# A two-block network on one core: transfers and first splits in another order, layer norm about a provisional mean, attention's last steps by head

## The chip, the cores and the metric

The kernel runs on one core of one Trainium2 chip. The metric is the device time in microseconds of one execution; the median over the runs is what is compared.

## The reference, cut to what matters

Input `x` is 256 tokens by 1024 features, in float32. Three stages follow one another: a block with a Conformer convolution, a SwiGLU feed-forward and a gated side input; a block with differential attention, feed-forward and side input; and a third block with a spatial gate, a pooling branch and a short convolution. All matrices are multiplied as split products (below). The change touches the first input norm, the convolution's layer norm and the end of attention:

```python
def layer_norm(x, g, b):
    mu = jnp.mean(xf, axis=-1, keepdims=True)
    xc = xf - mu
    var = jnp.mean(xc * xc, axis=-1, keepdims=True)
    y = xc * lax.rsqrt(var + EPS) * g + b
def conformer_conv(x, w_pw1, b_pw1, dw_w, dw_b, ln_g, ln_b, w_pw2, b_pw2):
    a = x @ w_pw1 + b_pw1
    u = a[..., :D_MODEL] * jax.nn.sigmoid(a[..., D_MODEL:])
    u = causal_depthwise_conv_31_taps(u, dw_w) + dw_b
    u = jax.nn.silu(layer_norm(u, ln_g, ln_b))
    return u @ w_pw2 + b_pw2
# attention, per head: w = softmax_0 - lam * softmax_1;  out = w @ v;  rms_norm(out) @ w_o
```

## The kernel before, in words

**Weights.** 169 pieces of 1 MB (128 partitions x 2048 float32) are streamed by SyncE into the four buffers `raw` (loop at L235 to L240). A piece `g` may be loaded when the split of piece `g-4` is done. Each piece is split in two parts: ScalarE writes `w_hi` (rounded to fp32r, `feed`, L936) and VectorE writes `w_lo = raw - w_hi` (L1424); GpSimd does this for the pieces in `POOL_LO` (`low`, L818). Each product is three TensorE matmuls, hi*hi, hi*lo and lo*hi (`mm3`, L282 to L284). `ahead` and `feed` write the order of the splits out by hand between the other steps of ScalarE and VectorE; each engine runs its instructions in program order and waits on semaphores.

**Start.** SyncE issues the two loads of `h` (the input, one per 128 tokens, L234) and then the weight pieces. ScalarE issues the load of `prm` (all per-feature parameters), squares `h` for the norm (L1065), GpSimd computes the factor (L805, L806), ScalarE scales the first half of the tokens (L1069) and VectorE the second (L1584). ScalarE then issues the two loads of `p_feat`. TensorE fills its wait with 23 dummy matmuls (`keep_busy`, L456), transposes the scaled tokens (L324), VectorE applies the gain (L1469), ScalarE and VectorE split it in `x_hi` (L954) and `x_lo` (L1479). Piece 0 is split in halves: first half `w_hi` by ScalarE (L1073), `w_lo` by VectorE (L1588); second half by ScalarE (L1075) and GpSimd (L825). The product `first_piece` has two halves in the same way, over features 0 to 511 and 512 to 1023.

**Convolution.** Features 0 to 511 (four blocks) are convolved on VectorE (31 instructions a block, `taps_on_vector`), with sums in bank 6; the other four on TensorE (`conv_taps`, L499), from rows spread through memory. The results are `y[:, 0..7, :]`, features on partitions, tokens along the row.

**Layer norm.** The mean over features is a matmul with the constant matrix `inv_d` (1/1024 everywhere): the sum of blocks 0, 1, 2 and 4 (`y_part`, made by GpSimd, L844 to L849) goes first (L522), blocks 5, 6, 3, 7 follow one by one (`mean_of`, L509). VectorE subtracts the mean from all blocks, two at a time (L1650); ScalarE squares them (L1143); eight matmuls on quadrants sum the squares (L536), VectorE copies (L1654), two matmuls of one column make the variance (L544), VectorE adds epsilon (L1657), GpSimd takes the power -1/2 (L865), VectorE makes diagonals (L1660), TensorE spreads them in a row (L550), VectorE multiplies (`scaled`, L1666), ScalarE applies Silu and rounds (L1151, L1156), VectorE forms `z_lo` (`v_split`, L1674), and `by_feature` begins the product with `pw2`. Four parts of the side input's projection (`projection_part`, 6 matmuls each) and six `keep_warm` transposes (L449) stand between these steps on TensorE. GpSimd, in the order of its program: splits of pieces 8, 9 and 10 with the sums for `y_part`, four additions of the bias row to `h` (L857), the store of the attention bias `toep` (L862), then the power.

**Attention's end.** For head `hd`: `logits`, VectorE `masked` (L1739) and `mix` (L1747 to L1754), ScalarE's exponentials (L1209), transposed weights (`weights`, L614) that ScalarE copies (L1215), and `values` for a pair of heads (L629 to L631), which VectorE evacuates (L1761). Squares of the outputs (L1229), GpSimd's power (L893, L894), `o_norm`, transposes (`o_jobs`), and the splits (L1236, L1780) go ahead of the product with `wo`.

Of the kernel before, what the change touches and what calls it, by code (L numbers as in the profile page):

```python
# [15 lines left out]
P = 128  # L16
# [61 lines left out]
def build(nc, ws, x_tok, p_feat, par, rows, lam_rows, rel, onehot, sgu_w, pool_m, toep, u_scr, out):  # L78
    ctx = ExitStack()
    with ctx:  # L80
# [174 lines left out]
        def _(pe):  # L255
# [93 lines left out]

            def projection_part(layer, g, b, t, n):  # L350

                begin(b)
                for k in range(2):
                    c = slice(k * D + n * 512, k * D + (n + 1) * 512)
                    ins = mm3(banks[b][:, :], tok(z_hi, KB - 2 + k, t), tok(z_lo, KB - 2 + k, t),
                              w_hi[:, g % SPLIT, c], w_lo[:, g % SPLIT, c], k == 0, k == 1)
                end(("proj", layer, t, n), b, ins, g if t == 1 and n == 1 else None)
# [101 lines left out]
            keep_busy(23, 7)  # L459
# [43 lines left out]
            def mean_of(f, last=False):  # L503

                if f < CONV_PE:
                    pe.wait_ge(S("conv"), f + 1)
                else:
                    pe.wait_ge(S("conv_pe"), f - CONV_PE + 1)
                ins = pe.matmul(banks[0][:, 0:SEQ], inv_d, y[:, f, :], start=False, stop=last)  # L509
                if last:  # L510
                    end("mean", 0, ins, release=(S("centred"), 4))
# [21 lines left out]
            for f in range(KB):  # L533
                pe.wait_ge(S("y_sq"), f // 2 + 1)
                j = f % QUADS
                ins = pe.matmul(banks[7][j * LANE:(j + 1) * LANE, 0:SEQ], inv_d[:, 0:LANE], sq[:, f, :],  # L536
                                start=f < QUADS, stop=f >= QUADS)
            end("squares", 7, ins, release=(S("y_sums"), 1))
            pe.wait_ge(S("y_sums"), 1)
            pe.wait_ge(S("one_32nd"), 1)  # L540
            begin(3)
            begin(2)
            for t, b in enumerate((3, 2)):
                end(("var", t), b, pe.matmul(banks[b][:, 0:1], y_sums[:, t * P:(t + 1) * P], one_32nd, start=True, stop=True),  # L544
                    release=(S("y_var"), t + 1))
            projection_part(0, G["proj0"], 5, 1, 0)
# [5 lines left out]
            projection_part(0, G["proj0"], 6, 1, 1)  # L552
            keep_warm(6, 7)
# [64 lines left out]
            def values(pair):  # L618

                def go():  # L620
# [32 lines left out]
            for step in (values(0), weights(5), weights(6), values(1), weights(7), values(2), values(3)):  # L653
                step()
# [129 lines left out]
        def _(pool):  # L784
# [11 lines left out]
            pool.memset(inv_d, 1.0 / D).then_inc(S("consts"), 1)  # L796
            pool.memset(u_pad[:, :, TAPS - 1 + SEQ:PADDED], 0.0)
# [4 lines left out]
            pool.dma_start(lam_t[:, :, :], bass.AP(lam_rows.tensor, 0, [[0, P], [HD, 4], [1, HD]])).then_inc(S("ld_lam"), 16)  # L802

# [11 lines left out]
            def low(g):  # L815
# [7 lines left out]
            pool.wait_ge(S("first_lo_a"), 1)  # L823
            pool.wait_ge(hi_done, 1)
            pool.tensor_tensor(w_lo[:, 0, D:HALF], raw[:, 0, D:HALF], w_hi[:, 0, D:HALF].bitcast(F32), ALU.subtract) \  # L825
                .then_inc(S("first_lo_b"), 1)
            pool.wait_ge(lo_done, 1)
# [26 lines left out]
            for n_ in range(2):  # L854
                for t in range(TT):
                    c = slice(n_ * 512, (n_ + 1) * 512)
                    pool.tensor_tensor(h[:, t, c], h[:, t, c], row_b2[:, c], ALU.add).then_inc(S("h_biased"), 1)  # L857


            pool.wait_ge(S("bias_row"), 2)  # L860
            pool.wait_ge(S("ld_u0"), 128)
            pool.dma_start(toep, bias_row[:, :].unsqueeze(1).to_broadcast([HEADS, P, 384])).then_inc(S("toep_out"), 16)  # L862
            pool.memset(one_32nd, 1.0 / LANE).then_inc(S("one_32nd"), 1)
            pool.wait_ge(S("y_var"), 2)
            pool.tensor_tensor(st[:, 84:86], st[:, 82:84], st2[:, 56:58], ALU.pow).then_inc(S("y_r"), 1)  # L865
            pool.wait_ge(S("h_done"), 4)
# [59 lines left out]
        def _(act):  # L926
# [133 lines left out]
            act.dma_start(prm[:, :], par).then_inc(S("ld_par"), 16)  # L1060
# [15 lines left out]
            fed[0] = 1  # L1076
            feed(1)
            h_split("x", 1)
            feed(2)

            def sigmoid(f):

# [1048 lines left out]
```

## Time and profile before

| | |
|---|---|
| runs | 1038.81, 1035.30, 1035.13 us; median 1035.3 |
| profiled execution | 1035.07 us, of which the span is 1033.3 |
| TensorE busy | 1022.6 us (99%) |
| VectorE / ScalarE / GpSimd busy | 638.0 / 517.7 / 109.5 us |
| chain that ended last | TensorE 97% of it |
| read from memory | 187.58 MB, 185 GB/s over the span |

A TensorE row of the timeline is a group of matmuls; a float32 matmul shows as two records (x2). Busy time of TensorE overlaps from one matmul to the next, so that starts are more telling than durations. "[0.65 <-DVE ...]" at the end of a row is the idle time of that engine before it, and what ended it.

### The profile page before, as it was taken

How to read it: one execution, taken by the hardware profiler on the slowest of the kernel's cores; microseconds unless marked ns; L12 is line 12 of the kernel's file. 1: busy time of each engine (PE TensorE's matmuls, PEld its weight loads, DVE VectorE, ACT ScalarE, POOL GpSimd, SP SyncE). 2: the span in 40 equal slices, each digit the busy share in tenths (PEclk: the TensorE clock that was granted, in tenths of full speed). 3: DMA queues.
4: the chain of work that ended last, by engine and by line, in shares of the span. 5: the costliest groups of instructions: out<-in, count | busy, mean ns of one | idle time of the engine just before them, and what ended most of it. 6: DMA issues, size and time to landing. Idle time of an engine off the chain costs nothing.

```text
span 1033.3 us, 13513 instructions
## 1 busy us (share of the span) xinstructions
PE 1022.6 (99%) x5510; PEld 864.1 (84%) x5510; DVE 638.0 (62%) x802; ACT 517.7 (50%) x635; POOL 109.5 (11%) x88
## 2 busy tenths in 40 slices
PE   8999999999999999999999999999999999999997
PEld 8977888888888888888888888788888888999886
DVE  5996654545557667765555456676454557777564
ACT  5437544343466668653444446754544453344433
POOL 4991100000020320010000002100000000000000
PEclk9999999999999999999999999999999999999999
DMA  8865865554543632565555544655555445554531
GB/s 322 247 220 102 276 229 169 197 203 167 200 163 139 228 122 82 204 242 187 196 172 201 190 177 163 228 207 197 193 189 183 158 164 204 180 187 166 204 120 41
DMA packets 30669, 191.67 MB, mean 186 GB/s; under 512 B 3720, under 2 KB 6280, under 8 KB 8720
## 3 DMA queue, kind: packets, MB, share of 16 engines
q1 hardware_dynamic: 25056, 179.06, 48.3%
q0 software_dynamic: 2096, 7.79, 3.3%
q10 hardware_dynamic: 3456, 3.97, 1.4%
q8 instruction: 44, 0.72, 0.3%
q14 instruction: 17, 0.14, 0.0%
HBM read 187.58 MB, written 3.21 MB: 185 GB/s over the span
## 4 chain that ended last, share of the span: by engine, by line
PE 97%; DMA 1%; ACT 1%; DVE 1%; issue 0%; POOL 0%; SPq 0%; POOLq 0%; ACTq 0%
PE bank L282 30%; PE bank L284 30%; PE bank L283 30%; PE bank L324 2%; PE bank L499 1%; PE bank L399 1%; DMA raw<-in_ws 1%; PE bank L593 0%; PE bank L690 0%; PE bank L727 0%; PE bank L614 0%; PE bank L509 0%; ACT arena L1209 0%; PE bank L594 0%; ACT w_hi L936 0%
## 5 line engine op out<-in xcount | busy, mean ns | idle before, releaser
L1424 DVE TENSOR_TENSOR w_lo<-raw,w_hi 128x2048 fp32r<-128x2048 f32 x157 | 359.3, 2291 | 209.8 <-ACT w_hi L936 208.2
L936 ACT ACTIVATE w_hi<-raw 128x2048 fp32r<-128x2048 f32 x168 | 320.9, 1910 | 161.6 <-PE bank L284 151.6
L282 PE MATMUL bank<-w_hi,x_hi 128*128 128x512 f32 x800 | 317.6, 397 | 0.2
L284 PE MATMUL bank<-w_hi,x_lo 128*128 128x512 f32 x800 | 312.4, 391 | 0.0
L283 PE MATMUL bank<-w_lo,x_hi 128*128 128x512 f32 x800 | 311.5, 389 | 0.0
L282 PEld LDWEIGHTS bank<-w_hi,x_hi 128*128 128x128 f32 x800 | 150.2, 188 | 34.3 <-issue 3.9
L284 PEld LDWEIGHTS bank<-w_hi,x_lo 128*128 128x128 f32 x800 | 150.2, 188 | 32.2
L283 PEld LDWEIGHTS bank<-w_lo,x_hi 128*128 128x128 f32 x800 | 150.4, 188 | 29.2
L282 PE MATMUL bank<-w_hi,z_hi 128*128 128x512 f32 (+1 forms) x368 | 143.5, 390 | 0.1
L284 PE MATMUL bank<-w_hi,z_lo 128*128 128x512 f32 (+1 forms) x368 | 141.8, 385 | 0.0
L283 PE MATMUL bank<-w_lo,z_hi 128*128 128x512 f32 (+1 forms) x368 | 141.6, 385 | 0.0
L282 PE MATMUL bank<-x_hi,w_hi 128*128 128x256 f32 x384 | 108.9, 284 | 0.3 <-DVE x_lo L1479 0.3
L283 PE MATMUL bank<-x_lo,w_hi 128*128 128x256 f32 x384 | 108.7, 283 | 0.0
L284 PE MATMUL bank<-x_hi,w_lo 128*128 128x256 f32 x384 | 108.7, 283 | 0.0
L818 POOL TENSOR_TENSOR w_lo<-raw,w_hi 128x2048 fp32r<-128x2048 f32 x11 | 50.8, 4625 | 359.5 <-ACT w_hi L936 356.0
L282 PEld LDWEIGHTS bank<-w_hi,z_hi 128*128 128x128 f32 x368 | 69.2, 188 | 14.2 <-issue 0.8
L284 PEld LDWEIGHTS bank<-w_hi,z_lo 128*128 128x128 f32 x368 | 69.1, 188 | 14.0
L283 PEld LDWEIGHTS bank<-w_lo,z_hi 128*128 128x128 f32 x368 | 69.2, 188 | 13.1
L282 PEld LDWEIGHTS bank<-x_hi,w_hi 128*128 128x128 f32 x384 | 73.7, 192 | 0.9 <-DVE x_lo L1479 0.4
L283 PEld LDWEIGHTS bank<-x_lo,w_hi 128*128 128x128 f32 x384 | 73.7, 192 | 0.0
L284 PEld LDWEIGHTS bank<-x_hi,w_lo 128*128 128x128 f32 x384 | 73.7, 192 | 0.0
L993 ACT ACTIVATE z_hi<-bank 128x512 fp32r<-128x512 f32 x22 | 13.1, 597 | 75.6 <-PE bank L399 75.6
(227 smaller groups left out, 757.4 us busy)
## 6 DMA issues: line engine op xcount, KB each, us to landing
raw<-in_ws SPq DMA_DIRECT2D x169, 1024.0 KB, 4.8
arena<-u_scr ACTq DMA_DIRECT2D x16, 142.0 KB, 5.6
arena<-in_rows POOLq DMA_DIRECT2D x2, 1024.0 KB, 4.7
toep<-bias_row POOLq DMA_DIRECT2D x1, 1536.0 KB, 35.4
h<-in_x_tok SPq DMA_DIRECT2D x2, 512.0 KB, 4.9
arena<-in_rows POOLq DMA_DIRECT2D x2, 512.0 KB, 5.4
arena<-toep POOLq DMA_DIRECT2D x1, 1024.0 KB, 9.2
arena<-in_pool_m POOLq DMA_DIRECT2D x1, 768.0 KB, 4.5
```

What stands on the lines that cost most here:

```text
L282: pe.matmul(dst, s_hi, m_hi, start=first, stop=False)
L283: pe.matmul(dst, s_hi, m_lo, start=False, stop=False)
L284: return pe.matmul(dst, s_lo, m_hi, start=False, stop=last)
L324: ins = pe.transpose(banks[b][:, k * P:(k + 1) * P], src[:, k * P:(k + 1) * P], ident[:, :])
L399: ins = pe.transpose(banks[b][:, k * SEQ + t * P:k * SEQ + (t + 1) * P], hid[:, t, k * P:(k + 1) * P], ident[:, :])
L499: ins = pe.matmul(banks[b][j * LANE:(j + 1) * LANE, 0:SEQ], taps_of[:, i, q, j, :], u_rows[i % 3][:, j, 4 * q:4 * q + SEQ], start=q == 0, ...
L818: pool.tensor_tensor(w_lo[:, g % SPLIT, :], raw[:, g % RAW, :], w_hi[:, g % SPLIT, :].bitcast(F32), ALU.subtract).then_inc(S("lo_pool"), 1)
L936: act.activation(w_hi[:, g % SPLIT, :], raw[:, g % RAW, :], ACT.Copy).then_inc(hi_done, 1)
L993: act.activation(z_hi[:, k0:k0 + 2, :], bank[:, :].rearrange("p (k s) -> p k s", k=2), ACT.Copy).then_inc(S("t_hi"), 1)
L1424: dve.tensor_tensor(w_lo[:, g % SPLIT, :], raw[:, g % RAW, :], w_hi[:, g % SPLIT, :].bitcast(F32), ALU.subtract).then_inc(lo_done, 1)
```

## The change

Transfers: `prm` is loaded by SyncE behind `h` and no longer by ScalarE; piece 0 is loaded in two halves; `lam_t` (GpSimd's queue) and `p_feat` (ScalarE's) are loaded later. First splits: ScalarE splits both halves of piece 0 in another order, and GpSimd makes the first half's `w_lo` too. Layer norm: a pivot (twice the mean over blocks 0, 1, 2, 4, by a matmul with `inv_half` = 2/1024) is subtracted from each block early, mostly by GpSimd; the squares are taken of these shifted values; the sum of the shifted blocks gives the remaining mean `e` (one column matmul for each half of the tokens, and one row matmul), the variance is corrected by `e*e`, and `e` is subtracted later, between the other steps. Attention: `values` waits for each head's copy by itself, and the last steps alternate.

```diff
@@ views
+        pivot_row = y_odd[:, 0, :]
+        inv_half = view(17408, P)
-        sq = view(6384, KB, SEQ)
+        sq = view(0, KB, SEQ)
@@ SyncE
-            for g in range(NPIECE):
+            sp.dma_start(prm[:, :], par).then_inc(S("ld_par"), 16)
+            sp.dma_start(raw[:, 0, 0:D], ws[0][:, 0:D]).then_inc(S("raw_first"), 16)
+            sp.dma_start(raw[:, 0, D:HALF], ws[0][:, D:HALF]).then_inc(raw_loaded[0], 16)
+            for g in range(1, NPIECE):
@@ TensorE
-            keep_busy(23, 7)
+            keep_busy(19, 7)
...
-            pe.matmul(banks[0][:, 0:SEQ], inv_d, y_part, start=True, stop=False)
-            mean_of(5)
+            end("pivot", 0, pe.matmul(banks[0][:, 0:SEQ], inv_half, y_part, start=True, stop=True),
+                release=(S("shifted_v"), 2))
             conv_taps(7)
-            mean_of(6)
-            mean_of(3)
-            mean_of(7, last=True)
...
-            for n in range(2):
-                projection_part(0, G["proj0"], (1, 4)[n], 0, n)
+            projection_step(0, G["proj0"], 1, 0, 0, 0)
+            projection_step(0, G["proj0"], 1, 0, 0, 1)
             begin(7)
+            square_of(0, 1)
+            square_of(1, 1)
+            square_of(2, 2)
+            square_of(4, 3)
+            square_of(5, 3)
+            square_of(6, 4)
+            square_of(3, 5)
+            square_of(7, 6, last=True)
+            begin(0)
+            pe.wait_ge(S("late_total"), 1)
+            for t in range(TT):
+                ins = pe.matmul(banks[0][:, t:t + 1], y_part[:, t * P:(t + 1) * P], inv_d[:, 0:1], start=True, stop=True)
+            end("e_cols", 0, ins, release=(S("e_sq"), 1))
+            begin(3)
             pe.wait_ge(S("y_sums"), 1)
...
+            end("mean", 2, pe.matmul(banks[2][:, 0:SEQ], inv_d, y_part, start=True, stop=True), release=(S("centred"), 4))
+            projection_step(0, G["proj0"], 4, 0, 1, 0)
+            projection_step(0, G["proj0"], 4, 0, 1, 1)
...  (y_row)
-            projection_part(0, G["proj0"], 6, 1, 1)
-            keep_warm(6, 7)
+            projection_step(0, G["proj0"], 5, 1, 0, 0)
+            projection_step(0, G["proj0"], 5, 1, 0, 1)
+            projection_step(0, G["proj0"], 6, 1, 1, 0)
+            projection_step(0, G["proj0"], 6, 1, 1, 1)
+            keep_warm(2, 7)
...  (values)
-                    pe.wait_ge(S("w_copied"), 2 * pair + 2)
                     for i in range(2):
                         hd = 2 * pair + i
+                        pe.wait_ge(S("w_copied"), hd + 1)
...
-            for step in (values(0), weights(5), weights(6), values(1), weights(7), values(2), values(3)):
+            for step in (values(0), weights(5), values(1), weights(6), values(2), weights(7), values(3)):
@@ GpSimd
-            pool.dma_start(lam_t[:, :, :], bass.AP(lam_rows.tensor, 0, [[0, P], [HD, 4], [1, HD]])).then_inc(S("ld_lam"), 16)
...
-            pool.wait_ge(S("first_lo_a"), 1)
+            pool.wait_ge(S("first_hi"), 1)
+            pool.tensor_tensor(w_lo[:, 0, 0:D], raw[:, 0, 0:D], w_hi[:, 0, 0:D].bitcast(F32), ALU.subtract) \
+                .then_inc(S("first_lo_a"), 1)
             pool.wait_ge(hi_done, 1)
...  (w_lo of the second half, then lam_t's load)
+            pool.memset(one_32nd, 1.0 / LANE).then_inc(S("one_32nd"), 1)
             low(10)
+            pool.wait_ge(S("pivot_row"), 1)
+            shift(0, 2)
+            shift(2, 3)
+            pool.wait_ge(S("conv_pe"), 2)
+            shift(4, 6)
+            pool.wait_ge(S("conv_pe"), 3)
+            shift(6, 7)
+            pool.wait_ge(S("shifted"), 4)
+            pool.tensor_tensor(y_part, y[:, 5, :], y[:, 6, :], ALU.add).then_inc(S("late_sum"), 1)
...  (toep's store)
+            add_b2(0, 0)
+            pool.wait_ge(S("y_var"), 1)
             pool.tensor_tensor(st[:, 84:86], st[:, 82:84], st2[:, 56:58], ALU.pow).then_inc(S("y_r"), 1)
+            pool.wait_ge(S("y_diag"), 2)
+            add_b2(0, 1)
+            add_b2(1, 0)
+            add_b2(1, 1)
@@ ScalarE
-            act.dma_start(prm[:, :], par).then_inc(S("ld_par"), 16)
...  (x_s of the first tokens)
+            act.wait_ge(S("raw_first"), 16)
+            act.activation(w_hi[:, 0, 0:D], raw[:, 0, 0:D], ACT.Copy).then_inc(S("first_hi"), 1)
+            h_split("x", 0)
+            act.wait_ge(raw_loaded[0], 16)
+            act.activation(w_hi[:, 0, D:HALF], raw[:, 0, D:HALF], ACT.Copy).then_inc(hi_done, 1)
+            fed[0] = 1
+            h_split("x", 1)
+            feed(2)
             act.dma_start(p_t0, p_feat[0]).then_inc(S("ld_p0"), 16)
             act.dma_start(p_t1[:, :, :], p_feat[1]).then_inc(S("ld_p1"), 16)
...
+            bank, _ = take(act, "pivot")
+            act.activation(pivot_row, bank[:, 0:SEQ], ACT.Copy).then_inc(S("pivot_row"), 1)
             conv_out(5)
             conv_out(6)
+            square(0, 2, (S("shifted"), 1))
+            square(2, 3, (S("shifted"), 2))
             conv_out(7)
+            square(4, 6, (S("shifted"), 3))
+            square(6, 7, (S("shifted"), 4))
+            square(3, 4, (S("shifted_v"), 1))
+            square(7, 8, (S("shifted_v"), 2))
+            bank, _ = take(act, "e_cols")
+            act.activation(st2[:, 50:52], bank[:, 0:TT], ACT.Square).then_inc(S("e_sq"), 1)
@@ VectorE
-            dve.wait_ge(S("first_hi"), 1)
-            dve.tensor_tensor(w_lo[:, 0, 0:D], raw[:, 0, 0:D], w_hi[:, 0, 0:D].bitcast(F32), ALU.subtract) \
-                .then_inc(S("first_lo_a"), 1)
...  (blocks 3 and 7 shifted from the bank, each y[:, f, :] -= bank)
+            dve.wait_ge(S("late_sum"), 1)
+            dve.wait_ge(S("shifted_v"), 2)
+            link(dve.tensor_tensor(y_part, y_part, y[:, 3, :], ALU.add))
+            dve.tensor_tensor(y_part, y_part, y[:, 7, :], ALU.add).then_inc(S("late_total"), 1)
...  (y_sums, variance; centre(i) subtracts e from blocks 2i and 2i+1)
-            for i in range(3):
-                scaled(i)
+            centre(0)
...  (diagonals, y_row)
+            scaled(0)
+            scaled(1)
+            centre(1)
             v_split(0)
+            scaled(2)
+            centre(2)
+            v_split(1)
             scaled(3)
-            v_split(1)
+            centre(3)
             scaled(4)
```

## Rows read from the trace of the kernel before

**Rows 1.** The page: TensorE's busy time, and the chain that ended last.
```profile
PE 1022.6 (99%) x5510; PEld 864.1 (84%) x5510; DVE 638.0 (62%) x802; ACT 517.7 (50%) x635; POOL 109.5 (11%) x88
PE 97%; DMA 1%; ACT 1%; DVE 1%; issue 0%; POOL 0%; SPq 0%; POOLq 0%; ACTq 0%
```
**Rows 2.** Waits of TensorE in the whole span: total us, times, longest.
```profile
PE bank L614 <- DVE arena L1754: 0.7, 1, 0.7
...
PE bank L324 <- DVE arena L1469: 0.4, 1, 0.4
```
**Rows 3.** Chain of waits at the start, and a DMA issue: size, us to landing.
```profile
1.63 9.35 DMA raw<-in_ws
...
lam_t<-in_lam_rows POOLq DMA_DIRECT2D x1, 128.0 KB, 7.5
```
**Rows 4.** Timeline of TensorE at the start: start us, us, instructions.
```profile
2.08 5.27 PE L456 MATMUL bank<-ident,ones 128*128 128x128 f32 x23 [2.08 <-POOL arena L798]
...
6.72 3.54 PE L456 MATMUL bank<-ident,ones 128*128 128x128 f32 x25
...
18.03 0.36 PE L282 MATMUL bank<-x_hi,w_hi 128*128 128x256 f32 x1 [0.26 <-DVE x_lo L1479]
```
**Rows 5.** Timeline of ScalarE, VectorE and GpSimd at the start.
```profile
6.55 1.06 ACT L1065 ACTIVATE arena<-h 128x1024 f32<-128x1024 f32 x1 [0.27 <-DMA h<-in_x_tok]
8.90 1.15 ACT L1069 ACTIVATE arena<-h,st 128x1024 f32<-128x1024 f32 x1 [1.20 <-POOL st L806]
...
12.09 1.22 DVE L1588 TENSOR_TENSOR w_lo<-raw,w_hi 128x1024 fp32r<-128x1024 f32 x1
13.23 1.29 DVE L1479 TENSOR_TENSOR x_lo<-arena,x_hi 128x512 fp32r<-128x512 f32 x2
...
14.21 2.57 POOL L825 TENSOR_TENSOR w_lo<-raw,w_hi 128x1024 fp32r<-128x1024 f32 x1 [5.41 <-ACT w_hi L1075]
```
**Rows 6.** VectorE's `x_lo` (ns min/median/max), and both engines' timeline in attention.
```profile
L1479 DVE TENSOR_TENSOR x_lo<-arena,x_hi x20: 677/691/932, 13.2 to 659.1; 128x512 fp32r<-128x512 f32 x20
...
338.27 2.29 DVE L1424 TENSOR_TENSOR w_lo<-raw,w_hi 128x2048 fp32r<-128x2048 f32 x1
338.42 2.21 POOL L888 TENSOR_SCALAR arena<-st 128x16 f32<-128x16 f32 x1 [9.45 <-DVE st L1719]
...
348.42 0.21 POOL L888 TENSOR_SCALAR arena<-st 128x16 f32<-128x16 f32 x1 [4.80 <-DVE st L1719]
```
**Rows 7.** Timelines of TensorE, GpSimd and VectorE in the layer norm.
```profile
76.87 1.68 PE L509 MATMUL bank<-arena 128*128 128x256 f32 x6
...
81.24 1.17 PE L536 MATMUL bank<-arena 128*32 128x256 f32 x16
82.94 0.61 PE L544 MATMUL bank<-st,arena 128*128 128x1 f32 x4 [0.53 <-DVE arena L1654]
...
88.07 0.47 PE L282 MATMUL bank<-w_hi,z_hi 128*128 128x512 f32 x1
...
69.01 0.73 POOL L849 TENSOR_TENSOR arena<-arena 128x256 f32<-128x256 f32 x1
...
74.23 4.98 POOL L857 TENSOR_TENSOR h<-h,arena 128x512 f32<-128x512 f32 x4
...
76.94 0.42 DVE L1633 TENSOR_TENSOR arena<-bank,arena 128x256 f32<-128x256 f32 x1
78.59 2.48 DVE L1650 TENSOR_TENSOR arena<-arena,bank 128x512 f32<-128x512 f32 x4 [1.22 <-PE bank L509]
...
87.54 0.43 DVE L1674 TENSOR_TENSOR z_lo<-arena,z_hi 128x256 fp32r<-128x256 f32 x1 [0.26 <-ACT z_hi L1156]
```
**Rows 8.** Timelines of TensorE and VectorE at attention's end.
```profile
406.65 0.55 PE L614 MATMUL bank<-ident,arena 128*128 128x128 f32 x3
...
414.94 1.40 DVE L1780 SCALAR_TENSOR_TENSOR z_lo<-bank,st,z_hi 128x512 fp32r<-128x512 f32 x2
...
416.11 0.39 PE L282 MATMUL bank<-w_hi,z_hi 128*128 128x512 f32 x1
```

More of the change, by code:

```diff
@@ L348, in ready_from, with projection_step @@
                 return ready
+            def projection_step(layer, g, b, t, n, k):
+                if k == 0:
+                    begin(b)
+                c = slice(k * D + n * 512, k * D + (n + 1) * 512)
+                ins = mm3(banks[b][:, :], tok(z_hi, KB - 2 + k, t), tok(z_lo, KB - 2 + k, t),
+                          w_hi[:, g % SPLIT, c], w_lo[:, g % SPLIT, c], k == 0, k == 1)
+                if k == 1:
+                    end(("proj", layer, t, n), b, ins, g if t == 1 and n == 1 else None)
             def projection_part(layer, g, b, t, n):
-                begin(b)
                 for k in range(2):
[L354 to L357, printed above, removed]
+                    projection_step(layer, g, b, t, n, k)
             def projection(layer, g, bank, between=None):
@@ L501, in conv_taps, with square_of @@
                 end(("conv", f), b, ins, release=(S("conv_pe"), i + 1))
[L503 to L509, printed above, removed]
+            def square_of(f, squared, last=False):
+                pe.wait_ge(S("y_sq"), squared)
+                j, second = {0: (0, 0), 3: (0, 1), 1: (1, 0), 7: (1, 1), 2: (2, 0), 5: (2, 1), 4: (3, 0), 6: (3, 1)}[f]
+                ins = pe.matmul(banks[7][j * LANE:(j + 1) * LANE, 0:SEQ], inv_d[:, 0:LANE], sq[:, f, :],
+                                start=not second, stop=bool(second))
                 if last:
-                    end("mean", 0, ins, release=(S("centred"), 4))
+                    end("squares", 7, ins, release=(S("y_sums"), 1))
             for f in (0, 4, 1, 5, 2, 6):
@@ L532, in _ @@
+            projection_step(0, G["proj0"], 1, 0, 0, 1)
             begin(7)
[L533 to L538, printed above, removed]
+            square_of(0, 1)
+            square_of(1, 1)
+            square_of(2, 2)
@@ L539, in _ @@
+            square_of(4, 3)
[9 more added lines that the diff above has]
+            begin(3)
             pe.wait_ge(S("y_sums"), 1)
             pe.wait_ge(S("one_32nd"), 1)
-            begin(3)
+            for t in range(TT):
+                ins = pe.matmul(banks[3][:, t:t + 1], y_sums[:, t * P:(t + 1) * P], one_32nd, start=True, stop=True)
@@ L542, in _ @@
+            end("var", 3, ins, release=(S("y_var"), 1))
             begin(2)
[L543 to L546, printed above, removed]
+            end("mean", 2, pe.matmul(banks[2][:, 0:SEQ], inv_d, y_part, start=True, stop=True), release=(S("centred"), 4))
+            projection_step(0, G["proj0"], 4, 0, 1, 0)
@@ L826, in _ @@
                 .then_inc(S("first_lo_b"), 1)
+            pool.dma_start(lam_t[:, :, :], bass.AP(lam_rows.tensor, 0, [[0, P], [HD, 4], [1, HD]])).then_inc(S("ld_lam"), 16)
             pool.wait_ge(lo_done, 1)
@@ L1654, in _, with centre @@
             dve.tensor_copy(y_sums, bank[:, 0:SEQ]).then_inc(S("y_sums"), 1)
-            for t in range(TT):
-                bank, free = take(dve, ("var", t))
-                dve.tensor_scalar(st[:, 82 + t:83 + t], bank[:, 0:1], 1.0, EPS, ALU.mult, ALU.add).then_inc(S("y_var"), 1)
+            def centre(i):
+                k = slice(2 * i, 2 * i + 2)
+                dve.tensor_tensor(y[:, k, :], y[:, k, :], e_bank[:, 0:SEQ].unsqueeze(1).to_broadcast([P, 2, SEQ]),
+                                  ALU.subtract).then_inc(S("centred"), 1)
+            bank, free = take(dve, "var")
+            dve.wait_ge(S("e_sq"), 1)
+            dve.scalar_tensor_tensor(out=st[:, 82:84], in0=bank[:, 0:TT], scalar=EPS, in1=st2[:, 50:52], op0=ALU.add,
+                                     op1=ALU.subtract).then_inc(S("y_var"), 1)
+            e_bank, _ = take(dve, "mean")
+            dve.wait_ge(S("shifted"), 4)
+            centre(0)
             dve.wait_ge(S("y_r"), 1)
```

46 lines of the change are left out of this document (19 added, 27 removed).

## The prediction

> **What bounds the kernel now.** The page comes first: TensorE is busy 99% of the span and 97% of the chain that ended last [rows 1]. So a change can only win where TensorE stands still, or where it does work that can go. The waits of TensorE over the whole span are few: the largest sum is 0.7 us, in attention, and the next 0.5 and 0.4 [rows 2, 7]. What remains lies at the start, where it does dummy work until inputs arrive. The chain of waits there shows piece 0 landing 9.35 us after its issue [rows 3], then splits, until the second half of `first_piece` begins at 18.03 [rows 4]. From there on every shift of TensorE passes on to the end, as long as nothing else becomes late. The three places of the change are therefore summed by the start of TensorE's next work in each. The profiled execution took 1035.07, 0.2 under the median of 1035.3; the sum is made against the first and the median shifted by it.
>
> **Start, transfers.** `prm` (257 KB) goes behind `h` (1 MB) and no longer beside it, and `lam_t` leaves GpSimd's queue for later (its small packets took 7.5 us to land [rows 3]). The square of the second `h` waited 0.27 us for its load [rows 5]. I take 0.4 us for how much earlier the scaled tokens come (bounds 0 and 1.0, one square). They then end at 9.65, not 10.05 [rows 5], and piece 0's first half has landed by then, as half of the 1 MB is asked for ahead of the rest. The extra issue on SyncE and `prm`'s (moved ahead of all pieces) delay pieces 1 to 3 by under 1 us each; they are used from 15 us on, so nothing. `p_feat`'s two issues follow `feed(2)` on ScalarE, whose next step, the first sigmoid, waits for TensorE; nothing. `lam_t`'s issue stands between the first split and `low(2)` on GpSimd, which waits for VectorE's split of piece 1 until 20 us; nothing.
>
> **Start, splits.** ScalarE's `w_hi` first half now ends at 10.7. GpSimd then makes `w_lo` in 2.57 [rows 5], until 13.2 to 13.3; VectorE did it in 1.22 until 13.3 [rows 5]. So the weights of the first half are no earlier. VectorE, freed of it, would want to form `x_lo` at 11.6, as both inputs are there. But here two engines meet: the longest `x_lo` took 932 ns, not 691 [rows 6]; it is the one at 16.40, while GpSimd's `w_lo` ran to 16.78 [rows 5]. And a GpSimd instruction of 16 columns took 2.21 us, not 0.21, when VectorE's `w_lo` ran beside it: it ended with it, at 340.6 [rows 6]. So one waits for the whole of the other when VectorE reads two operands from memory. `x_lo` has two (`arena`, `x_hi`); it will start at 13.2, where it starts now (13.23 [rows 5]). The Trainium skill says so too (SBUF — State Buffer, Who interferes with whom: a VectorE instruction with two SBUF inputs contends with a GpSimd instruction that reads SBUF), and its page Perfetto Trace Analysis (Optimizing Scalar/DVE Operations) warns that moving work between the two may not help; the rows above carry the sum without it.
> Next GpSimd wants the second half (ready at 13.2), and VectorE has its second `x_lo` queued. If VectorE goes first, `x_lo` ends at 14.5, as now (13.23 + 1.29), GpSimd runs 14.4 to 16.8, the third `x_lo` starts at 16.8 and the fourth ends at 18.1: the second half begins at 18.1 against 18.03. Start: 0. The bounds: without any blocking, `x_lo` is ready at 12.9, `w_lo` at 13.2 and 15.8, TensorE comes through its transposes, bias and five dummies at 14.1, and the second half begins at 17.1: 0.9 gained, 1.5 if the fillers do not hold it. If GpSimd goes first, it is 1.9 lost (below). `keep_busy` loses four matmuls: 38 passes instead of 46. The first 23 took 5.27 us, the last 25 3.54 [rows 4], so the 38 end near 9.3, before the tokens at 9.65. No cost; the dummies cover nothing but the clock.
>
> **Layer norm.** TensorE work removed: four mean matmuls; three took 1.68 [rows 7], so 2.1 with their overlap taken off. Four `keep_warm` transposes, at the 0.14 us of the later passes in [rows 4] at most, 0.5. The waits of 0.53 [rows 7] and 0.2 (the row matmul's). Added: the two column matmuls, priced as those of the variance, 0.6 [rows 7], and one row matmul, 0.5. A longer wait: GpSimd ends `low(10)` at 74.23 [rows 7]; the pivot is ready by then (`y_part` 69.74, matmul and copy until 73.4). Four shifts of 512, 256, 512 and 256 columns and a sum of 256 cost 1.25, 0.73, 1.25, 0.73, 0.73 (4.98/4 and 0.73 [rows 7]), to 79.0 with gaps. VectorE adds two blocks of 0.42 [rows 7], to 80.0. TensorE comes there at: 76.5 (0.4 earlier, one mean matmul less ahead of `conv_taps(7)`), a projection part 1.4, squares 1.15 [rows 7] = 79.1. New wait 0.9. Squares by ScalarE and VectorE's two shifts (block 3 done at 77.4 [rows 7]) finish at 79.5 beside this. Afterwards the copy of the sums, the power, `centre(0)` (a quarter of 2.48 [rows 7]) and the diagonals lie beside the variance, mean and projection matmuls. Net: -2.1 -0.5 -0.7 +1.1 +0.9 = -1.3, so `pw2` starts at 86.8, not 88.07 [rows 7]. What is late next: `centre(1)` and `centre(2)`, 0.6 each, now stand between VectorE's steps, and `z_lo` of the third block of features comes at 90.0, needed at 89.6: 0.4 back. `v_split(0)` (87.54 now [rows 7], 85.5 then) has two memory operands and meets `add_b2` on GpSimd, which moved behind the diagonals (83.1 to 86.9): 0.1 if it gets in between. Layer norm: -0.8. Bounds: -2.1 (no new wait at all), +0.4 (`v_split(0)` behind all of `add_b2`, to 87.3, and the third block with it). The toep store keeps its time; `h_biased` is needed at 100, nothing.
>
> **Attention.** The 0.7 [rows 2] before `weights(6)` and about 0.3 before `weights(7)` go: `values(1)` and `values(2)` need no late copy. `weights(7)` is transposed at 406.9, not 406.65 [rows 8], and ScalarE is busy until 407.2 anyway. TensorE reaches the projection 1.0 earlier. But the product with `wo` needs `z_lo`, which VectorE forms from 414.94 on, 0.70 for the first half [rows 8], after `o_norm` and a weight split whose chain the change doesn't shorten. TensorE starts there at 416.11 [rows 8] and could at 415.7. So 0.4 stays (bounds 0 and 1.0).
>
> **Sum:** 0 - 0.8 - 0.4 = -1.2, so 1033.9 for a profiled execution and 1034.1 for the median. 0.5% is 5.2 us, about what a measurement of this kernel can tell from no change; the forecast lies within it.
>
> **Rivals.**
> *No blocking that counts.* VectorE's `x_lo` starts at 11.6, `v_split` on time: -0.9 -0.9 -0.4, up to -0.6 more for attention: 1032.8. For it: most VectorE forms here read one operand from a bank. Against: [rows 6]. Chance 0.22.
> *GpSimd keeps the port* (the other side: slower). Place: between the first and second `x_lo`. GpSimd's second half runs 13.8 to 16.3, the second `x_lo` ends at 17.0, the first half of `first_piece` runs 17.0 to 19.9, and the second starts at 19.9 instead of 18.03: +1.9. With `v_split(0)` behind `add_b2` (+0.4) and attention's -0.4 it is +1.9: 1037.2. It decides from the point where the second `x_lo` starts after 16. Chance 0.19, since no row shows who wins when both wait.
> *TensorE's clock falls.* The passes of 128 columns went from 0.23 us each to 0.14 within the dummies [rows 4], that is from the lower to the higher level, 1.2 to 2.4 GHz. Fewer dummies and a longer gap at 14 to 17 us could bring it down again: the first piece's 48 matmuls (0.12 each now) at half speed cost 5.8 more: 1041. For it: only together with the rival above is the gap much over the 0.4 of [rows 2], after which no matmul was slower. [...] Chance 0.05.
> *The change doesn't do what it says* for the mean: if the pivot were late, every square would be. GpSimd is busy with `low(10)` until 74.23 while the pivot is there at 73.4, so this is priced already.
>
> **How the numbers follow.** Forecast 0.50, no blocking 0.22, GpSimd first 0.19, clock 0.05, a gain over 5.2 us from an effect I don't see 0.04 (all gains at their bounds are 1.5 + 2.1 + 1.0 = 4.6). Faster by over 0.5%: 0.04. Slower: 0.05, and 0.01 of the third case. Within: 0.90. The range goes from 1031.8 (bounds of the start and attention in the second case) to 1037.4 (the third case).
>
> **What would show it.** Start: the third matmul group of `first_piece` (its second half) near 18.1, `x_lo` starting at 13.2 right at GpSimd's end, or at 11.6 (second case), or its second at 16.3 (third). Layer norm: a wait of 0.9 for `late_total` ahead of the column matmuls, `pw2` 1.3 earlier relative to `conv_taps(7)`, a wait of 0.4 within it. Attention: both waits at L614's place gone, new ones before the output transposes or `wo`. Wrong it would be if TensorE waits for a split of the weights during the convolution, or if rows before 18 us shift by over 2.

## The result and the profile after

The changed kernel takes **1040.8 us** (median of 5, 1040.5 to 1041.4) against 1035.3 for the kernel before (1035.1 to 1038.8): ratio 1.0048, 95% interval 1.0036 to 1.0061. It is 5.5 us slower. The forecast was 1034.1 in a range of 1031.8 to 1037.4; the time lies above it. The profiled execution took 1040.79 with a span of 1038.7, so 5.7 more than that of before.

First the page, as in [rows 1]: TensorE is busy 1.7 us longer than before (1022.6), though it has 14 instructions fewer.
```profile
PE 1024.3 (99%) x5496; PEld 865.6 (83%) x5496; DVE 643.4 (62%) x804; ACT 519.0 (50%) x639; POOL 116.7 (11%) x95
PE 91%; POOL 5%; DVE 2%; ACT 1%; DMA 0%; issue 0%; POOLq 0%; ACTq 0%; SPq 0%; DVEq 0%
```
The waits of TensorE (total us, times, longest) have two new ones, of 2.3 and 1.9 us. The largest before was 0.7 [rows 2], apart from 2.1 us ahead of the first dummy, which both kernels have and [rows 2] leaves out:
```profile
PE bank L287 <- DVE x_lo L1532: 2.3, 1, 2.3
...
PE bank L551 <- DVE arena L1704: 1.9, 1, 1.9
```
**Start.** VectorE's and GpSimd's timelines, in the order of [rows 5]:
```profile
11.26 4.88 DVE L1532 TENSOR_TENSOR x_lo<-arena,x_hi 128x512 fp32r<-128x512 f32 x2
...
10.49 2.36 POOL L842 TENSOR_TENSOR w_lo<-raw,w_hi 128x1024 fp32r<-128x1024 f32 x1 [2.61 <-ACT w_hi L1111]
12.85 2.75 POOL L845 TENSOR_TENSOR w_lo<-raw,w_hi 128x1024 fp32r<-128x1024 f32 x1
```
The first two `x_lo` took 1.29 us together before; now they take 4.88. The first began at 11.26, waited for GpSimd's first half (to 12.85) and took 2.14; the second began at 13.3, waited for the second half (to 15.60) and took 2.83. GpSimd got in between two instructions that VectorE had ready. TensorE's timeline and the table by stretch (us, busy times of PE, PEld, DVE, ACT, POOL, then granted clock, DMA share, GB/s) show what followed:
```profile
9.18 1.09 PE L329 MATMUL bank<-ident,arena 128*128 128x128 f32 x8 [0.61 <-ACT arena L1109]
...
12.60 1.38 PE L467 MATMUL bank<-ident,ones 128*128 128x128 f32 x10
16.25 0.46 PE L287 MATMUL bank<-x_hi,w_hi 128*128 128x256 f32 x1 [2.27 <-DVE x_lo L1532]
16.51 0.41 PE L288 MATMUL bank<-x_lo,w_hi 128*128 128x256 f32 x1
16.72 0.41 PE L289 MATMUL bank<-x_hi,w_lo 128*128 128x256 f32 x1
```
```profile
15.00:18.00 3.00, 1.75 (x8) 1.78 (x9) 2.90 (x4) 1.22 (x3) 1.16 (x2) 0.72 0.96 347
...
80.00:87.00 7.00, 5.09 (x33) 3.79 (x32) 3.86 (x6) 3.57 (x9) 4.53 (x5) 0.83 0.67 178
87.00:90.00 3.00, 3.00 (x10) 2.42 (x9) 1.08 (x3) 0.69 (x2) 1.79 (x2) 0.50 0.43 51
```
After the 2.27 us gap the matmuls of 256 columns stand 0.21 us apart instead of 0.12: the granted clock is at the lower of its two levels (1.2 of 2.4 GHz) until 19.7. VectorE's first tap of the convolution starts 2.6 later than before; the line of the kernel before comes first:
```profile
21.84 0.48 DVE L1607 SCALAR_TENSOR_TENSOR arena<-bank,prm,arena 128x256 f32<-128x256 f32 x1 [1.06 <-ACT arena L1088]
```
```profile
24.44 0.49 DVE L1657 SCALAR_TENSOR_TENSOR arena<-bank,prm,arena 128x256 f32<-128x256 f32 x1 [1.67 <-ACT arena L1128]
```
In the kernel before, the clock was 1.00 in 80 to 87 and in 87 to 90 us; now it is 0.83 and 0.50.

**Layer norm.** TensorE, VectorE and GpSimd, in answer to [rows 7]:
```profile
75.99 3.66 PE L510 MATMUL bank<-arena 128*32 128x256 f32 x64 [0.48 <-issue]
...
84.34 0.75 PE L551 MATMUL bank<-arena 128*128 128x1 f32 x4 [1.91 <-DVE arena L1704]
...
87.24 0.63 PE L288 MATMUL bank<-w_lo,z_hi 128*128 128x512 f32 x1
87.66 0.63 PE L289 MATMUL bank<-w_hi,z_lo 128*128 128x512 f32 x1
...
93.70 0.48 PE L287 MATMUL bank<-w_hi,z_hi 128*128 128x512 f32 x1
```
```profile
81.54 0.42 DVE L1703 TENSOR_TENSOR arena<-arena 128x256 f32<-128x256 f32 x1 [0.70 <-POOL arena L892]
82.00 2.19 DVE L1704 TENSOR_TENSOR arena<-arena 128x256 f32<-128x256 f32 x1
...
81.46 1.15 POOL L895 DMA_DIRECT2D toep<-bias_row  x1
82.63 1.27 POOL L875 TENSOR_TENSOR h<-h,arena 128x512 f32<-128x512 f32 x1
```
The second of VectorE's two late additions takes 2.19 us instead of 0.42: it ends at 84.2, right behind `add_b2(0, 0)` (83.9). TensorE waits 1.91 for it, and then its clock falls a second time: 512 columns stand 0.43 us apart (0.23 at the higher level) until 91.3. `pw2` starts at 93.70, 5.6 later than before (88.07), so the layer norm costs 3.0 (5.6 less the start's 2.6) where 0.8 was to be won.

**Attention.** The 0.7 before `weights(6)` is gone, 0.15 before the output transposes is new. The product with `wo` starts at 421.56, +5.45 [rows 8]: 0.2 won.

### The profile page after: what moved, and what is told of

It reads as the page before. It is cut to its first block, busy times and chain, and to the rows that moved or that the text cites. A ratio compares the mean times of both kernels' runs of the same rounds, so it can differ in the third digit from the quotient of the medians.

```text
span 1038.7 us, 13501 instructions
## 1 busy us (share of the span) xinstructions
PE 1024.3 (99%) x5496; PEld 865.6 (83%) x5496; DVE 643.4 (62%) x804; ACT 519.0 (50%) x639; POOL 116.7 (11%) x95
## 4 chain that ended last, share of the span: by engine, by line
PE 91%; POOL 5%; DVE 2%; ACT 1%; DMA 0%; issue 0%; POOLq 0%; ACTq 0%; SPq 0%; DVEq 0%
PE bank L287 29%; PE bank L289 29%; PE bank L288 29%; POOL w_lo L836 3%; PE bank L329 2%; PE bank L410 1%; POOL arena L828 1%; DVE x_lo L1532 0%; PE bank L612 0%; DMA h<-in_x_tok 0%; DVE bank L1677 0%; POOL arena L879 0%; PE bank L709 0%; PE bank L746 0%; ACT arena L1282 0%
## 5 line engine op out<-in xcount | busy, mean ns | idle before, releaser
L288 PEld LDWEIGHTS bank<-w_lo,z_hi 128*128 128x128 f32 x368 | 69.6, 189 | 13.3
```

Source lines behind the costliest of these rows:

```text
L288: pe.matmul(dst, s_hi, m_lo, start=False, stop=False)
```

## The experiments

Each ran in turn with the kernel before, whose median was 1035.2 to 1035.3 each time. "After" is the changed kernel, 1040.8. Some kernels spread over several us from one execution to the next; where they do, the spread is given, and the median is only as good as it allows. The kernel before was more than 2 us above its fastest in 13 of its 109 executions beside the experiments.

### One port collision at the start taken away
```
             pool.wait_ge(hi_done, 1)
+            pool.wait_ge(S("x_split"), 2)
             pool.tensor_tensor(w_lo[:, 0, D:HALF] ...
```


> The changed kernel with one wait more: GpSimd begins the second half of piece 0's w_lo only after VectorE has made both x_lo of the first half. Theory (GpSimd takes the port between two queued VectorE instructions): the two x_lo end near 14.1 us instead of 16.14, first_piece starts near 14.3 instead of 16.25 and its matmuls are 0.12 us apart, not 0.21, as the gap that let the clock fall is gone; its second half starts near 17.9. pw1 and all behind it come 2.6 to 2.8 us earlier, so about 1038.1 us. Rival (the clock fell because of the fewer dummies, whatever VectorE does): the matmuls stay 0.21 apart for about 16 of them and the time stays above 1039. Rival (transfers late): nothing moves, 1040.8.

**1038.2** (ratio 1.0029, 1.0017 to 1.0041), -2.6, as expected. The seven executions run from 1036.2 to 1040.5, though (after: 1040.5 to 1041.4), and the profiled one took 1039.9, so the median mixes the gain with something else. Its VectorE and GpSimd:
```profile
12.04 3.13 DVE L1533 TENSOR_TENSOR x_lo<-arena,x_hi 128x512 fp32r<-128x512 f32 x2 [0.75 <-ACT x_hi L996]
...
15.31 2.42 POOL L846 TENSOR_TENSOR w_lo<-raw,w_hi 128x1024 fp32r<-128x1024 f32 x1 [1.29 <-DVE x_lo L1533]
```
The pair takes 3.13 and ends at 15.2, with only the first half ahead of it (this profile's first split is 1.2 later than after's), and TensorE's matmuls start 0.12 apart. The profile shows a wait nobody had foreseen too, which comes back below: 3.35 us for the spread rows before `conv_taps(7)`, the matmuls of the convolution's last block:
```profile
77.20 6.30 PE L510 MATMUL bank<-arena 128*32 128x256 f32 x64 [3.35 <-issue]
```
A price of the mend without that wait comes from the run with both orders mended (below): its first tap starts at 22.16, 2.3 before after's 24.44.

### The layer norm's collision taken away
```
-            add_b2(0, 0)
             pool.wait_ge(S("y_var"), 1)
 ...
             pool.wait_ge(S("y_diag"), 2)
+            add_b2(0, 0)
             add_b2(0, 1)
```


> The changed kernel with GpSimd's first bias addition to h moved from ahead of the power to behind the diagonals, so that it isn't on the port while VectorE adds the late blocks. Theory (the second add waited for that instruction): the add that took 2.19 us takes 0.42, or up to 1.0 if the issue of the toep store alone holds the port until 82.6; TensorE's wait of 1.91 for it becomes 0.2 to 0.8, the clock stays at its higher level in the layer norm, and pw2 starts 3 to 4 us earlier: 1036.8 to 1038. Rival (the clock falls because of the short matmuls and waits that are left): the add is short, but the matmuls of 84 to 91 us stay 0.43 apart and the gain is 1.2 to 1.8, about 1039.3. Rival (the port has nothing to do with it): 1040.8.

**1036.8** (1.0013, 1.0004 to 1.0022; ten executions, 1035.6 to 1037.8), -4.0, as expected. Both additions are short, with GpSimd's issue of a DMA beside them, which did not lengthen them:
```profile
81.47 0.42 DVE L1702 TENSOR_TENSOR arena<-arena 128x256 f32<-128x256 f32 x1 [0.73 <-POOL arena L892]
81.93 0.42 DVE L1703 TENSOR_TENSOR arena<-arena 128x256 f32<-128x256 f32 x1
...
81.39 1.15 POOL L895 DMA_DIRECT2D toep<-bias_row  x1
```
TensorE reaches its column matmuls at 82.50 instead of 84.34 and keeps the clock at 1.00.

### The clock alone at the start
```
-            keep_busy(5, 7)
+            keep_busy(15, 7)
```


> The changed kernel with 15 dummy matmuls instead of 5 ahead of first_piece, which fill the gap of 13.7 to 16.25 us; VectorE and GpSimd as they are. This prices the clock alone. Theory (the clock fell for lack of work in that gap): first_piece still starts at 16.2 to 16.4, but its matmuls are 0.12 apart from the first; everything behind comes 1.4 us earlier, 1039.4 us. Rival (the two halves of the loss are all port): no change, 1040.8, with matmuls 0.21 apart.

**1039.4** (1.0041, 1.0027 to 1.0056), -1.4, as expected, from four executions. `x_lo` is blocked as in after and ends even later in this profile (16.90; after 16.14), but TensorE idles only 0.68 us:
```profile
12.71 3.62 PE L467 MATMUL bank<-ident,ones 128*128 128x128 f32 x30
17.00 0.36 PE L287 MATMUL bank<-x_hi,w_hi 128*128 128x256 f32 x1 [0.68 <-DVE x_lo L1532]
17.20 0.28 PE L288 MATMUL bank<-x_lo,w_hi 128*128 128x256 f32 x1
17.32 0.28 PE L289 MATMUL bank<-x_hi,w_lo 128*128 128x256 f32 x1
```
So of the start's loss 1.4 is the clock. The idle time made it fall, and not the fewer dummies ahead of the transposes, which this run has too.

### Each part alone on the kernel before
Attention (waits and order of steps only):

> The kernel before with only the attention edit. As predicted: TensorE reaches the projection 1.0 us earlier, waits up to 0.2 for the output norm and starts wo where VectorE's z_lo is ready, 0.4 us earlier than before: 1034.9 us. Rival (nothing else is late): 1034.3. Rival (no gain): 1035.3.

**1035.3** against 1035.2 (1.0005, 0.9995 to 1.0014): the rival, no gain that can be measured. The trace of after gives 0.2.

The start alone (transfers, splits, dummies):

> The kernel before with only the start of the change: transfers, order of the first splits, GpSimd's first half, 19 dummies. Theory (the start alone costs the 2.6 us by which the pivot came late): the second x_lo ends near 16.1 us, the matmuls of first_piece begin at 16.25 and are 0.21 apart up to 19.7, the pivot's sibling (the mean's first matmul) comes at 74.8 instead of 72.2, and the time is 1037.6 to 1037.9. Rival (the loss arises in the layer norm alone): 1035.2.

**1038.35** (1.0031, 1.0019 to 1.0044; the fastest of five 1038.2), +3.0, 0.5 above what was expected. In the profiled execution (1039.4, the slowest) TensorE waits 3.19 us for `x_lo` and the clock falls: the matmuls from 17.1 to 22.2 us are the slow ones.

The layer norm alone, as the change has it:

> The kernel before with only the layer norm of the change, with the bias addition where the change puts it. Theory: the second late add takes 2.19 us again, TensorE waits 1.9 for it, the clock falls between 84 and 89 us of this kernel's own time, and pw2 starts 3.3 us later than 88.07: 1038.5. Rival (the layer norm suffers only because it comes late after the slow start): the add takes 0.42, and the time is 1033.5 to 1034.5.

**1036.9** (1.0009, 0.9999 to 1.0018), its runs in two groups, near 1035.6 and near 1037.2. Both expectations missed: mine was 1.6 too high, the rival's too low. The profiled run, of 1037.5, has the 2.19 us addition and the clock at 0.76 in 80 to 87 us. The four runs near 1035.6 were not profiled. Their mean granted clock is 0.998, that of the six others 0.996 to 0.997, and 1035.6 is what the mended layer norm of the next run (1033.9) gives with 1.8 of blocking and no fall added. So the clock probably held in them, but that isn't shown.

### The old start with the mended layer norm and attention
The start of the kernel before; `add_b2(0, 0)` behind the diagonals.

> The start of the kernel before, with the layer norm and the attention of the change and GpSimd's first bias addition behind the diagonals. Theory: pw2 starts at 86.4 to 86.9 instead of 88.07 (a wait of 0.5 within it for z_lo comes on top), attention gives 0.2: 1033.8 us, which would beat both kernels. Rival (the layer norm of the change gains nothing even with the port free): 1035.0 to 1035.3.

**1033.9** (0.9992, 0.9983 to 1.0000), as expected, eight of 11 runs below 1034.4. That is 1.4 under the kernel before by the medians, though the interval just reaches no change: layer norm and attention are sound but for the place of one addition.

### The transfers put back
The same, with the change's transfers and its order of ScalarE's first splits; VectorE splits the first half, GpSimd's second half waits for two `x_lo`, 23 dummies.

> As e7, with the transfers of the change too (parameters on SyncE, piece 0 in halves, later loads of the rest), 23 dummies, VectorE making the first half's w_lo, and GpSimd beginning the second half only after both first x_lo. Theory: the tokens come 0.9 us earlier than before, x_lo of the first half ends at 13.6 to 14.3, GpSimd's half at 16.0 to 16.7, and the second half of first_piece starts at 17.3 to 18.0 instead of 18.03: 1033.1 to 1033.8 us. Rival (piece 0 lands so late that the earlier tokens bring nothing, or the gap ahead of first_piece lets the clock fall): 1034 to 1036.

**1036.6** (1.0004, 0.9994 to 1.0014), spread from 1033.7 to 1038.1: the theory missed, and the median lies even above the rival's 1034 to 1036. ScalarE began to scale the tokens at 7.88, but TensorE was in its dummies until 10.4. The profiled execution (1034.5) doesn't explain the spread.

### After, with both orders mended

> The changed kernel with both orders mended: GpSimd's second half of w_lo waits for the first two x_lo, and add_b2(0, 0) stands behind the diagonals. Theory (two port collisions, each with its clock fall, and nothing else, make the change slow): the gains of the two single mends add up, -2.6 and -4.0, so 1040.8 - 6.6 = 1034.2, with the granted clock at its higher level from 15 us on. Rival (the parts share a cost, such as one clock fall that either mend takes away; or the second pair of x_lo, blocked by GpSimd's half, is a loss of its own): the gains overlap, 1036 or more. If the whole change were sound but for the two orders, it would be at the -0.8 -0.4 of the forecast: 1034.

Median **1034.8** (1.0002, 0.9990 to 1.0014). Six of 12 runs are at 1034.1 to 1034.4, where the two gains add up (1034.2); the others reach 1040.2. So the two collisions with their clock falls are the whole loss of the change, whose own executions all lie within 1 us, and with them gone something else comes and goes.

### The clock alone in the layer norm
After, with seven dummies ahead of the wait for `late_total`.

> The changed kernel with seven dummy matmuls (14 passes, some 1.7 us at the higher level) ahead of TensorE's wait for late_total. They take the place of the 1.9 us wait and make nothing ready earlier: the addition of 2.19 us stays. Theory (of the 4.0 that the other place of add_b2(0, 0) gave back, 1.75 are the blocked addition and the rest the clock after the gap): the projection's matmuls are 0.21 us apart and not 0.43, the granted clock stays up at 85 to 91 us, and the time is 1040.8 - 2.2 = 1038.6. Rival (the whole loss is the wait, and the slow matmuls have another cause): 1040.8 or a little more.

**1043.4** (1.0071, 1.0059 to 1.0083), +2.6 instead of -2.2: a miss, through my choice of the bank. The dummies went into bank 7, which was free only once VectorE had read the squares, behind the slow addition. They filled nothing and ran after the gap. The same into the free bank 0:

> As the run before it with seven dummy matmuls in the layer norm, but they write into bank 0, which is free, and not into bank 7: there they waited for VectorE to read the squares, which stands behind the slow addition, so they ran after the gap and did not fill it (2.14 us idle ahead of them, 2.15 us of dummies behind it). Now they run in the 1.9 us gap itself. Theory (1.75 of the 4.0 are the blocked addition, the rest is the clock after the gap): no fall of the granted clock at 85 to 91 us, projection matmuls 0.21 us apart, 1038.6. Rival (the clock falls for another cause, or the slow matmuls are no clock): 1040.8.

**1038.75** (1.0028, 1.0018 to 1.0038; nine executions, 1037.1 to 1039.9), -2.1, as expected. TensorE there (matmuls of 512 columns 0.23 apart afterwards; my 0.21 in the text was a slip), and the clock:
```profile
84.21 1.83 PE L550 MATMUL bank<-ident,ones 128*128 128x128 f32 x14
86.10 0.61 PE L553 MATMUL bank<-arena 128*128 128x1 f32 x4
...
85.00:88.00 3.00, 2.94 (x23) 2.62 (x22) 1.81 (x4) 1.24 (x2) 1.32 (x2) 1.00 0.56 55
```
VectorE's addition still takes 2.19. So the 4.0 of the layer norm are about 1.9 of blocking and 2.1 of clock, each with an uncertainty of some tenths, given the spread.

### The earlier tokens used, and a cause of the spread
The kernel of the transfers experiment with 19 dummies.

> The kernel before with the change's transfers, its layer norm with add_b2(0, 0) behind the diagonals, its attention, and 19 dummies at the start, but VectorE splitting the first half of w_lo as before and GpSimd's second half waiting for the first two x_lo. Theory (the tokens come 0.9 earlier than before, but with 23 dummies TensorE was not free for them): the transposes start at 9.2 instead of 10.4, and the second half of first_piece starts 0.3 to 0.8 earlier than in the kernel before: 1033.0 to 1033.8, below the 1033.9 of the old start. Rival (the transposes do not set when first_piece starts, since x_lo waits for w_lo on VectorE, and the fewer dummies bring the clock down more often): 1034.5 to 1036.6.

**1037.4** (1.0009, 0.9997 to 1.0022), above the theory and the rival; only two of 11 runs below 1034.1. The second half of `first_piece` began at 17.57, 0.46 earlier than in the kernel before, and yet the time is longer. ScalarE's queue, VectorE and TensorE of its profile tell why:
```profile
27.57 0.34 ACTq L1137 DMA_DIRECT2D u_scr<-arena  x1
...
32.28 2.78 ACTq L1146 DMA_DIRECT2D arena<-u_scr  x4
35.11 0.63 ACT L1090 ACTIVATE z_hi<-arena 128x512 fp32r<-128x512 f32 x1 [5.19 <-issue]
```
```profile
36.21 0.49 DVE L1658 SCALAR_TENSOR_TENSOR arena<-bank,prm,arena 128x256 f32<-128x256 f32 x1 [3.18 <-ACT arena L1126]
...
75.36 5.35 PE L510 MATMUL bank<-arena 128*32 128x256 f32 x64 [2.92 <-issue]
```
The first store of `u` took 4.7 us to land (2.0 before). ScalarE issues the reading back behind it, then `z_hi` and the sigmoid; VectorE's taps idle 3.18 us for that, the last `u` is late, and `conv_taps(7)` waits 2.92 for its rows. That gap brings the clock down as well (0.66 in 75 to 80 us): the 64 matmuls take 5.35 instead of 3.66. The profile of the first experiment has the same chain (5.2 us to land, a wait of 3.35). In both, `p_feat` and `lam_t` load late, as the change has it. Two runs told whether they do it. The first puts both loads back to their early places:

> The kernel of e11_transfers_19 with the loads of p_feat and lam_t back at their old, early places. In the profile of e11 the second half of first_piece began 0.5 earlier than before, yet the first store of u took 4.7 us to land (2.3 in e9_both, 2.0 before), ScalarE stood behind it until 32.3 us, VectorE's taps came 2.6 later, and conv_taps(7) waited 2.9 at 72 to 75 us: 1037.4. Theory (the late loads of p_feat and lam_t push the weight pieces into the moment of that store): without them the store lands in about 2 us, and the times are steady at 1033.0 to 1033.6. Rival (the moved prm and split first piece are enough, or the earlier start itself): as spread as e11, 1036 to 1037.5.

**1033.6** (0.9988, 0.9977 to 1.0000), 9 of 12 runs from 1033.0 to 1034.0: the lowest median of the study, 1.6 under the kernel before (the 0.3 under 1033.9 are within the noise). The other three reach 1038.9, so it isn't steady as expected. Its profile has the store at 3.4 us and a wait of 1.3, hardly more than the 1.2 of the kernel of 1033.9, whose store took 2.0. The second moves nothing but these two loads, in the steady kernel of 1033.9:
```
 ScalarE: -p_feat's two loads ahead of the first split   +behind feed(2)
 GpSimd:  -lam_t's load first                            +behind the second half of w_lo
```


> The kernel of e7_norm_mended, whose times were nearly all 1033.8 to 1033.9, with the loads of p_feat and lam_t moved to the late places of the change, and nothing else of the start. Theory (the late loads make the first store of u land late in many executions): a spread of times, 1034 to 1038, with a median over 1035. Rival (they are harmless by themselves): 1033.9 as before.

**1036.8** (1.0002, 0.9989 to 1.0016), 1033.6 to 1039.0, eight of 12 over 1035.8. The run of 1033.9 was taken at another time, so the fair comparison is with the two kernels measured together with this one: it was more than 2 us above its fastest in 8 of 12 executions, the one with early loads in 3 of 12, the kernel before in 5 of 23. Its profile shows the chain again, cut at 79 us by the view:
```profile
27.89 0.34 ACTq L1134 DMA_DIRECT2D u_scr<-arena  x1
...
32.31 3.30 ACTq L1143 DMA_DIRECT2D arena<-u_scr  x4
...
75.80 3.41 PE L507 MATMUL bank<-arena 128*32 128x256 f32 x36 [3.02 <-issue]
```
All 64 matmuls take 4.92 there, 1.26 more than the 3.66 of the kernel of 1033.9, and the wait is 1.9 longer (3.02 against 1.16): together 3.1. So the late loads cost about 3 us in most executions by themselves. They are no part of the 5.5: in after, where everything came 2.6 later, the store landed in 1.8. They are not the only source of such executions either, as the kernel before has some too. Why the store lands late is open. That the loads push the weight pieces into its way is argued, and the mean traffic does not decide it: in 26 to 34 us it was 300 to 301 GB/s in the two profiles shown here (4.4 and 4.7 us to land) and 211 in after (1.8), but 291 in the kernel before (2.0) and in the kernel of 1033.9 (2.0). Which of the three loads does it wasn't tried.

## Why the prediction was wrong, point by point

**Start, transfers: the tokens.** Forecast: scaled tokens 0.4 earlier. It is 0.9 (TensorE's transposes at 9.18 against 10.10), near the upper bound. "`p_feat`'s two issues follow `feed(2)`...; nothing" is the step that failed: I looked at who is queued behind the issues and who needs the data, not at what the loads do to the transfers after them. In after it cost nothing that shows, so it is no part of the 5.5; with the rest mended it costs 3 in most executions (1036.8 against 1033.9).

**Start, splits.** That the two engines exclude each other was right, in size too: `x_lo` began late by the whole of GpSimd's instruction. The step that failed is "If VectorE goes first, `x_lo` ends at 14.5". No row showed who wins when both have work ready, the text said so, and the forecast took the happier case at 0.50 against 0.19. GpSimd won in all six profiles that have this order (4.8 to 5.3 us for the pair of `x_lo`). In each its second half is recorded 0.4 to 0.5 before the second `x_lo` (12.85 and 13.3 in after): it was waiting already while VectorE's first ran. The prediction's own times had that too, GpSimd ready at 13.2 and the second `x_lo` due only at 13.9. Whether the order of asking decides was not tested by itself, and the layer norm below does not fit it by its recorded starts. The rival "GpSimd keeps the port" named the place; for its 1.9 the runs have 0.9 to 1.6 for the port alone (the first tap's 2.3, or the 3.0 of the start alone, less 1.4 for the clock).

**TensorE's clock.** Given 0.05, as an event by itself. But the rival of the port contained a gap of some 2 us on TensorE, and its price left the clock out. It fell wherever the port made TensorE wait for 1.9 us or more: the chances were not independent. Its size was far off as well: 5.8 was worked out for all 48 matmuls; it fell for some 3.5 us only and cost 1.4.

**Layer norm.** What failed is "VectorE adds two blocks of 0.42 [rows 7], to 80.0". I tested `v_split(0)` against `add_b2`, not the additions that stand right ahead of it, since GpSimd's `toep` issue was to lie between. It did by the profile, and the addition is blocked even so: 1.8, and 2.1 of clock behind it, in place of 0. `v_split(0)` was not delayed (0.43).

With that addition moved, layer norm and attention together came out at -1.4 by the medians (-1.2 forecast), `pw2` started at 86.86 (86.8 forecast) and the wait of 0.4 for `z_lo` was there as 0.5. But this agreement is partly luck, as the kernel of 1033.9 shows:
```profile
74.21 3.66 PE L507 MATMUL bank<-arena 128*32 128x256 f32 x64 [1.16 <-issue]
...
79.39 1.13 PE L515 MATMUL bank<-arena 128*32 128x256 f32 x16
80.45 0.61 PE L548 MATMUL bank<-arena 128*128 128x1 f32 x4
```
`conv_taps(7)`, forecast 0.4 earlier, waits 1.16 for its rows and starts 0.9 later than the 73.28 of before (0.48 waited in after). And the new wait of 0.9 for `late_total` isn't there: the column matmuls follow the squares without idle time. Two terms of about 1 us each were wrong and cancelled.

The Trainium skill's rule, which I quoted for the start (SBUF — State Buffer, Who interferes with whom), is that such instructions of the two engines contend; the trace agrees at both places (4.88 us for 1.29, 2.19 for 0.42). It was used at one.

**Attention.** 0.4 forecast, 0.2 in the trace, nothing in the times: `weights(6)` no longer waits, but the output transposes do.

**The sum.** By the trace, +2.6 for the start instead of 0, +3.0 for the layer norm instead of -0.8 and -0.2 for attention instead of -0.4 make 5.4; measured 5.5. (The start alone cost 3.0 as a kernel of its own.) Two rivals came true, the first at two places. The upper end of the range held the port once and without its clock; that is why 1037.4 was too low. Two slips in the text changed nothing: the largest wait of TensorE before was the 2.1 at the very start and not 0.7, and the second case's -2.2 from 1035.3 is 1033.1, not 1032.8.

## What to carry to other kernels

List every instruction of VectorE with two operands in memory and of GpSimd that can be ready in the same microseconds, at all places of a change, and price the overlap as one waiting for all of the other, with the order that hurts unless a semaphore or the program fixes it. Fixing it cost nothing that could be seen here: with both orders mended, half of the executions of the changed kernel took 1034.1 to 1034.4 instead of 1040.8. Where a wait of some 2 us or more falls on TensorE between short stretches of work, add the clock's fall to its price, or fill it with dummies into a bank that is free. A load moved to "later, where it is needed only much later" lands in someone's traffic: look for a small transfer there that a whole queue waits for (here a store of 144 KB).

## What the runs showed of the hardware

- Between two VectorE instructions with two memory operands that were both ready, a waiting GpSimd instruction took its turn: 4.88 us for two `x_lo` that took 1.29 before.
- VectorE's addition from 82.00 on, which takes 0.42 alone, was still blocked when GpSimd's instruction was recorded to begin, at 82.63 behind a DMA issue, and ended right behind it. The issue by itself blocked nothing (0.42 beside it, twice). So either the hold on the port began before the recorded start or that start is recorded late; no run tells which.
- In the profiles of this case the granted clock of TensorE fell after each of the twelve idle times from 1.91 to 3.35 us behind the first dummies (in the one of 2.19 only 0.8 us into the work that followed), and not after 0.68, 1.16 and 1.26. The line isn't sharp: in the profiled run of attention alone (1037.9, the slowest but one of its ten) it fell behind a wait of 1.31 for the tokens and eight transposes, with the start of the kernel before. That kernel has executions of this kind of time too, 1037.6 to 1037.9 with a mean granted clock of 0.995, in 8 of 109; they were not profiled. In after it stayed down for 3.5 us at the start and for 7 in the layer norm.
- The same 144 KB store landed in 1.8 to 5.2 us over the profiles.
